# Gate and up of six FFNs as seven block products instead of eight, on one core of a Trainium2 chip

## The chip, the core and the metric

The kernel runs on one core of a Trainium2 chip. TensorE multiplies matrices into PSUM, VectorE and ScalarE work on SBUF and PSUM, GpSimd does small things, SyncE issues the DMAs. Each engine runs its own queue of instructions in order, and they meet at semaphores. The metric is the device time of one execution in microseconds, the median of the runs.

## What is computed

Two transformer blocks over x of 512 tokens x 1024, in float32: nine stages, of which six are FFNs (1, 3, 4, 6, 7, 9) and three are mixers (2: pooling and attention, 5: gated convolution, 8: Fourier and grouped attention). d_ff is 2816 in stages 1 to 6 and 2752 in 7 and 9.

```python
def rms_norm(x, g):
    xf = x.astype(jnp.float32)
    y = xf * lax.rsqrt(jnp.mean(xf * xf, axis=-1, keepdims=True) + NORM_EPS)
    return (y * g.astype(jnp.float32)).astype(x.dtype)

def swiglu(x, w_gate, w_up, w_down):
    return (jax.nn.silu(x @ w_gate) * (x @ w_up)) @ w_down
...
        x = x + 0.5 * swiglu(rms_norm(x, ffn1_norm[layer]),
                             ffn1_w_gate[layer], ffn1_w_up[layer], ffn1_w_down[layer])
```

## The kernel before

x stays in SBUF transposed (`X`: 8 tiles k of 128 channels x 512 tokens). A float32 product is made from three products of the type fp32r (`mm3`, lines 423 to 425): each operand is split into a high part (ScalarE's rounding copy: `Xh`, `wh`, `Hh`) and a low part (VectorE's subtraction: `Xl`, `wl`, `Hl`), and low x high, high x low and high x high are summed in one PSUM bank. The row factor of the norm is applied after the product: ScalarE squares the tiles of X, VectorE sums the squares into `acc`, eight one-column matmuls (line 475) add over the channels, GpSimd takes the inverse root (`r4`), two matmuls (lines 487, 488) spread it over the partitions (`rb`).

Weights come as chunks of at most 128 x 1024 elements. `weight_stream` lists them in the order of use; SyncE loads chunk n into `raw[n % 3]`, ScalarE's `high()` (line 929) and VectorE's `low()` (line 1315) split it into `wh`, `wl`. `use()` in each engine's program counts the chunks that TensorE takes and keeps the split `AHEAD = 2` chunks in front of it; the split of chunk n waits until TensorE has used chunk n-3.

An FFN (`ffn` in each program) takes hidden columns in pairs of 128. For each pair, gate and up: weights stationary, X moving with 512 tokens, 8 k tiles. The hidden comes out transposed as down needs it. VectorE multiplies gate by `rb` (line 1325), ScalarE takes the silu (line 997), VectorE multiplies up by `rb` and both, ScalarE makes `Hh` (line 960) and VectorE `Hl`. Down (`residual`) then runs over 22 hidden tiles for the 8 tiles of X, in parts of 2, 2, 2, 1 and 1 tiles (`DOWN`); behind each tile VectorE adds to X (line 1328), ScalarE makes `Xh` (957), VectorE `Xl`, and the square is summed. After the attention mixers (`mixer_out`) the tiles 4 to 7 of X come close together and their squares are summed last.

All order is written out by hand: what stands first in an engine's program is done first. `HERE` is a wait of VectorE for all of its own earlier instructions. Transposes (`turn`, line 569) are four 128-column instructions on TensorE into one bank; before, only the mixers have them. `begin(s)` waits for all engines' end of the stage before.

## Time and profile before

| | |
|---|---|
| median of 3 runs | 2712.67 us (2712.37 to 2713.19) |
| span of the profiled execution | 2710.9 us |
| TensorE, weight loads | 99%, 83% of the span |
| VectorE, ScalarE, GpSimd | 49%, 33%, 5% |
| DMA | 252.8 MB, mean 93 GB/s |

The span runs from the first to the last instruction of the profiled execution, which is one execution of its own beside the timed ones. Matmuls are pipelined: a duration of 0.39 us covers entering and leaving the array, and the pace is the distance of two starts. Lines named with an instruction are often those of a helper.

### The profile page before, as it was taken

Reading aid. Unit: us, or ns where it says so; the run is one execution under the profiler, and the core shown is the slowest. Engines: PE = TensorE matmul, PEld = TensorE weight load, DVE = VectorE, ACT = ScalarE, POOL = GpSimd, SP = SyncE. Lnnn points to the kernel's source line nnn. Section 1 sums busy time; section 2 is a strip of 40 time slices with the busy share of each in tenths; the row PEclk is TensorE's granted clock in tenths of the full one; section 3 lists DMA queues with packets and bytes.
Section 4 is the critical chain, followed back from the end, with each engine's and each line's share of the span. In section 5 each row is a group of like instructions: output and inputs, shape, how many; then the busy total and the mean of one; then the engine's idle time right before and its main releaser. Section 6 shows DMA issues by size and latency. Waiting matters only on the chain.

```text
span 2710.9 us, 31115 instructions
## 1 busy us (share of the span) xinstructions
PE 2691.8 (99%) x12443; PEld 2243.5 (83%) x12443; DVE 1339.6 (49%) x1908; ACT 900.5 (33%) x1278; POOL 136.7 (5%) x133
## 2 busy tenths in 40 slices
PE   8999999999999999999999999999999999999998
PEld 7888888888888888888888888888888888888887
DVE  5444358764443444434565444334444478644433
ACT  4232236543222332322223322223222237433221
POOL 0000004400000000000000000000000044100000
PEclk9999999999999999999999999999999999999999
DMA  4332332133332333323333233233332321233332
GB/s 158 97 99 95 94 88 74 32 96 104 96 97 92 95 104 96 100 94 94 101 93 101 94 99 96 92 97 99 99 96 93 101 84 40 71 93 93 102 101 78
DMA packets 287088, 252.81 MB, mean 93 GB/s; under 512 B 12640, under 2 KB 283744, under 8 KB 286944
## 3 DMA queue, kind: packets, MB, share of 16 engines
q1 hardware_dynamic: 286944, 250.81, 30.3%
q8 instruction: 100, 1.64, 0.2%
q14 instruction: 44, 0.36, 0.0%
HBM read 248.68 MB, written 2.10 MB: 93 GB/s over the span
## 4 chain that ended last, share of the span: by engine, by line
PE 97%; DVE 2%; ACT 0%; issue 0%; DMA 0%; SPq 0%; POOLq 0%; POOL 0%; DVEq 0%
PE bank L423 32%; PE bank L424 32%; PE bank L425 32%; PE bank L569 1%; PE bank L475 0%; DVE wl L1315 0%; PE bank L627 0%; PE bank L628 0%; DMA X<-in_xT 0%; DVE a_mx L1435 0%; PE bank L431 0%; PE bank L432 0%; DVE ft L1325 0%; DVE Xl L1328 0%; ACT wh L929 0%
## 5 line engine op out<-in xcount | busy, mean ns | idle before, releaser
L1315 DVE TENSOR_TENSOR wl<-raw,wh 128x1024 fp32r<-128x1024 f32 (+2 forms) x486 | 571.1, 1188 | 915.0 <-ACT wh L929 914.5
L423 PE MATMUL bank<-Xh,wl 128*128 128x512 f32 x2528 | 988.0, 391 | 7.6 <-DVE wl L1315 6.7
L425 PE MATMUL bank<-Xh,wh 128*128 128x512 f32 x2528 | 984.9, 390 | 0.0
L424 PE MATMUL bank<-Xl,wh 128*128 128x512 f32 x2528 | 984.7, 390 | 0.0
L929 ACT ACTIVATE wh<-raw 128x1024 fp32r<-128x1024 f32 (+2 forms) x486 | 490.9, 1024 | 946.1 <-PE bank L425 941.0
L423 PEld LDWEIGHTS bank<-Xh,wl 128*128 128x128 f32 x2528 | 474.5, 188 | 109.3 <-ACT wh L929 6.3
L425 PEld LDWEIGHTS bank<-Xh,wh 128*128 128x128 f32 x2528 | 474.4, 188 | 100.2
L424 PEld LDWEIGHTS bank<-Xl,wh 128*128 128x128 f32 x2528 | 474.6, 188 | 97.8
L423 PE MATMUL bank<-Hh,wl 128*128 128x512 f32 (+1 forms) x1061 | 408.5, 385 | 0.0
L425 PE MATMUL bank<-Hh,wh 128*128 128x512 f32 (+1 forms) x1061 | 408.3, 385 | 0.0
L424 PE MATMUL bank<-Hl,wh 128*128 128x512 f32 (+1 forms) x1061 | 408.3, 385 | 0.0
L1325 DVE TENSOR_TENSOR ft<-bank,rb 128x512 f32<-128x512 f32 x264 | 181.5, 688 | 167.4 <-PE bank L425 106.9
L425 PEld LDWEIGHTS bank<-Hh,wh 128*128 128x128 f32 x1061 | 199.3, 188 | 40.0
L423 PEld LDWEIGHTS bank<-Hh,wl 128*128 128x128 f32 x1061 | 199.3, 188 | 39.7
L424 PEld LDWEIGHTS bank<-Hl,wh 128*128 128x128 f32 x1061 | 199.3, 188 | 39.6
L960 ACT ACTIVATE Hh<-ft 128x512 fp32r<-128x512 f32 x132 | 83.4, 632 | 265.0 <-DVE ft L1325 265.0
L997 ACT ACTIVATE ft<-ft 128x512 f32<-128x512 f32 x132 | 83.5, 632 | 209.3 <-DVE ft L1325 209.2
L1325 DVE TENSOR_TENSOR Hl<-ft,Hh 128x512 fp32r<-128x512 f32 x130 | 90.0, 692 | 90.8 <-ACT Hh L960 90.8
L1325 DVE TENSOR_TENSOR ft<-ft,ft 128x512 f32<-128x512 f32 x132 | 91.4, 692 | 4.5
L957 ACT ACTIVATE Xh<-X,par 128x512 fp32r<-128x512 f32 x64 | 46.1, 722 | 123.9 <-DVE X L1328 108.0
L1971 POOL TENSOR_TENSOR r<-small,half 128x4 f32<-128x4 f32 (+1 forms) x11 | 10.5, 956 | 1368.1 <-DVE small L1334 1368.1
L1328 DVE SCALAR_TENSOR_TENSOR Xl<-X,par,Xh 128x512 fp32r<-128x512 f32 x64 | 47.8, 750 | 38.4 <-ACT Xh L957 38.4
(295 smaller groups left out, 1547.9 us busy)
## 6 DMA issues: line engine op xcount, KB each, us to landing
raw<-in_ffn_w_up SPq DMA_DIRECT2D x130, 512.0 KB, 4.0
raw<-in_ffn_w_gate SPq DMA_DIRECT2D x129, 512.0 KB, 3.6
raw<-in_ffn_w_down SPq DMA_DIRECT2D x114, 512.0 KB, 3.4
raw<-in_c_w_in SPq DMA_DIRECT2D x24, 512.0 KB, 3.7
raw<-in_w_in SPq DMA_DIRECT2D x10, 512.0 KB, 4.0
raw<-in_a_w_in SPq DMA_DIRECT2D x8, 512.0 KB, 3.7
raw<-in_a_w_out SPq DMA_DIRECT2D x8, 512.0 KB, 3.4
raw<-in_c_w_out SPq DMA_DIRECT2D x8, 512.0 KB, 3.4
```

Of the source, the lines that this page charges most:

```text
L423: e.matmul(o, ll, rh, start=start, stop=False)
L424: e.matmul(o, lh, rl, start=False, stop=False)
L425: i = e.matmul(o, lh, rh, start=False, stop=stop)
L569: e.transpose(bank[0:rows, t * 128:(t + 1) * 128], src, ident).then_inc(mm.up(name), 1)
L929: e.activation(part_of(n, wh), part_of(n, raw), ACT.Copy).then_inc(whi.up(("w", n)), 1)
L957: e.activation(Xh[:, t, :], X[:, t, :], ACT.Copy, scale=col(gain, t)).then_inc(act.up(("xh", s, t)), 1)
L960: e.activation(dst, src, ACT.Copy, scale=scale).then_inc(act.up(*names), 1)
L997: e.activation(B[0:wd, :], A[0:wd, :], ACT.Silu).then_inc(act.up(("silu", s, ht)), 1)
L1315: e.tensor_tensor(part_of(n, wl), part_of(n, raw), part_of(n, wh).bitcast(F), ALU.subtract).then_inc(wlo.up(("w", n)), 1)
L1325: e.tensor_tensor(dst, a, b, op).then_inc(dve.up(*names), 1)
L1328: e.scalar_tensor_tensor(dst, a, scalar, b, op0, op1).then_inc(dve.up(*names), 1)
L1971: e.tensor_tensor(dst, a, b, op).then_inc(pool.up(*names), 1)
```

## The change

For 2560 of the hidden columns (`GROUPED`), gate and up are one product C = A B with A = tokens x channels and B = channels x (512 gate columns, 512 up columns), five groups. A and B are cut into 2 x 2 blocks (256 tokens x 512 channels; 512 channels x 512 columns) and C is made from seven block products, D, A, B, E, B2, E2 and A2, instead of eight. The left operands are S3, the plain first block, N2, S1, a plain block, S4 and a plain block: sums of quarters of X times the gain, built at the start of each FFN (`Sf`, split into `Sh` and `Sl`). The right operands are t3, B11, t2, t1/t4, B22, B21: t1 to t4 are sums of weight blocks which VectorE makes for each half of 256 channels (`add`). Two products add on to a bank that has been read before (`again`). The operand that moves is now the weight (512 columns), the stationary one the tokens, so the hidden comes out with tokens in the partitions: VectorE and ScalarE combine the products from PSUM (U1, U2, U3, C22, C21, C12), the row factor is a scalar of the partition (`r4`), and `rb` with its two spreading matmuls is dropped in FFNs. `turn_hidden` transposes the gated hidden in blocks of 128, two blocks before the end of gate and up and the others between the matmuls of the first part of down; `Hh` and `Hl` are made from its bank. The remaining 256 (192) columns a side come first (`rest`), ordinary products with 4 token subtiles.

A unit of weights is 256 channels x 512 columns, used by 2 token subtiles (a group has 14); units of the groups have a ring of four `wh`/`wl` slots and are split three ahead, sums two further; eight raw slots hold the loads, five of them in the area of the stage, which after a mixer waits for its end (`AFTER_MIXER`). `("used", u)` is signalled behind a unit's last matmul, a product's end behind each of its two banks. The stage-wide constants of ScalarE move behind stage 1's groups.

```diff
-N_RAW = 3
-AHEAD = 2
+N_RAW = 8
+N_RING = 4
+PLAIN = (0, 1, 2)
+GROUPED = 2560

...
-FIRST = ((0, 128), (128, 256), (256, 512), (512, 1024))
+FIRST = ((0, 128), (128, 256), (256, 512), (512, 768), (768, 1024))
+REST = ((0, 256), (256, 512), (512, 768), (768, 1024))
...
+def chunks_ffn(s, wg, wu, wd):
+
+
+    got = chunks_rest(wg, wu, FIRST if s == 1 else REST)
+    for n0 in range(0, GROUPED, 512):
+        blocks = {}
+        for kh in range(2):
+            for name, w, k0 in (("B11", wg, 0), ("B12", wu, 0), ("B21", wg, 512), ("B22", wu, 512)):
+                k = k0 + 256 * kh
+                blocks[name, kh] = ([(0, (0, 512), 0, rows_of(w, k, k + 256, n0, n0 + 512))], 512, 2)
+        got.append((s, n0 == 0, blocks))
+    return got + chunks_down(wd, wg.shape[1])
...
+LOADS = (("B22", 0), ("B12", 0), ("B22", 1), ("B12", 1), ("B11", 0), ("B11", 1), ("B21", 0), ("B21", 1))
+UNITS = ("t3", "B11", "t2", "t1", "t4", "B22", "B21")
+LAST_USE = {"B11": 6, "B12": 6, "B22": 10, "B21": 12}
+LEAD = 2
+AFTER_MIXER = (3, 6, 9)
...
+        for name in UNITS:
+            for kh in range(2):
+                b11, b12, b21, b22 = (("raw", raw[b, kh]) for b in ("B11", "B12", "B21", "B22"))
+                part = ("part", kh)
+                source, total = {
+                    "t3": (part, (b22, b12, ALU.subtract)), "t2": (part, (part, b11, ALU.add)),
+                    "t1": (b12, (b12, b11, ALU.subtract)), "t4": (part, (b21, part, ALU.subtract)),
+                    "B11": (b11, None), "B22": (b22, None), "B21": (b21, None)}[name]
+                unit(512, 2, range(N_RING), 3, source, total)
+    sums = {}
+    for n, got in enumerate(units):
+        if got.sum:
+            lead = LEAD if units[n - LEAD].ahead == 3 else 0
+            sums.setdefault(n - lead, []).append(n)
+    return loads, units, release, sums
 
...
+            def turn_hidden(s, k):
+
+                rows = last_block(s) if k == 21 else 128
+                bank = take(TURNS[k % 4], ("turn", s, k))
+                w.wait_ge(par_in, 16)
+                w.wait_ge(dve, ("h", s, k // 4))
+                for t in range(4):
+                    e.transpose(bank[0:rows, 128 * t:128 * t + 128], H[:, k, t, 0:rows], ident).then_inc(
+                        mm.up(("turn", s, k)), 1)
...
+            def product(s, g, into, name, lh, ll, kh0, column, start, between=None):
+
+
+                for kh in range(2):
+                    if kh and between:
+                        between()
+                    u, h, l, _ = chunk()
+                    for i in range(2):
+                        sl = slice(column + 128 * i, column + 128 * i + 128)
+                        for kk in range(2):
+                            k, end = kh0 + 2 * kh + kk, kh == 1 and kk == 1
+                            names = [("used", u)] if kk and i else []
+                            if end:
+                                names.append((name, s, g, i))
+                            mm3(into[:, i, :], lh[:, k, sl], ll[:, k, sl], h[:, kk, :], l[:, kk, :],
+                                start and kh == 0 and kk == 0, end, *names, again=not start)
...
             def ffn(s):
...
+                rest(s)
+
+                def made(j):
+                    w.wait_ge(act, ("Sh", s, j))
+                    w.wait_ge(dve, ("Sl", s, j))
+
+                def first_turns():
+                    turn_hidden(s, 0)
+                    turn_hidden(s, 1)
+
+                for g in range(5):
+                    made(0)
+                    product(s, g, take_pair(PD, ("D", s, g)), "D", Sh[0], Sl[0], 0, 0, True)
+                    product(s, g, take_pair(PA, ("A", s, g)), "A", Xh, Xl, 0, 0, True)
+                    made(1)
+                    product(s, g, take_pair(PB, ("B", s, g)), "B", Sh[1], Sl[1], 0, 0, True)
+                    made(2)
+                    product(s, g, take_pair(PE, ("E", s, g)), "E", Sh[2], Sl[2], 0, 0, True)
+                    product(s, g, take_pair(PB, ("B2", s, g)), "B2", Xh, Xl, 4, 256, True)
+                    made(3)
+                    product(s, g, take_pair(PE, ("E2", s, g)), "E2", Sh[3], Sl[3], 0, 0, False)
+                    product(s, g, take_pair(PA, ("A2", s, g)), "A2", Xh, Xl, 4, 0, False, first_turns if g == 4 else None)
...
+                    into = [take((4 + t) % 8, ("down", s, t)) for t in range(t0, t1)]
+                    k = 0
+                    while k < 22:
+                        u, h, l, nk = chunk()
+                        for kk in range(nk):
+                            if t0 == 0 and k + 2 < 22:
+                                turn_hidden(s, k + 2)
+                            w.wait_ge(act, ("hh", s, k))
+                            w.wait_ge(dve, ("hl", s, k))
+                            for i, bank in enumerate(into):
...
             def ffn(s):
+                n = f - GROUPED
+                use(2 if s == 1 else 1)
+                if s > 1:
+                    begin(s)
+                for k in range(4):
+                    if s > 1:
+                        w.wait_ge(dve, ("x", s - 1, 4 + k))
+                    copy(Sf[2][:, k, :], X[:, 4 + k, 256:512], ("half2", s, k), scale=gain_of(s, 4 + k))
+                use()
+                for k in range(4):
+                    w.wait_ge(dve, ("S3", s))
+                    copy(Sh[0][:, k, :], Sf[0][:, k, :], ("Sh", s, 0), scale=gain_of(s, k))
+                use()
+                w.wait_ge(dve, ("N2", s))
+                copy(Sh[1][:, :, :], Sf[1][:, :, :], ("Sh", s, 1))
+                use()
+                for t in range(4):
+                    w.wait_ge(mm, ("rest", s, t))
+                    w.wait_ge(pool, ("r4", s))
+                    e.activation(U2[:, t // 2, 256 * (t % 2):256 * (t % 2) + n], banks[(6, 7, 0, 1)[t]][:, 0:n], ACT.Silu,
+                                 scale=r4[s % 2][:, t:t + 1]).then_inc(act.up(("rest", s, t)), 1)
+                w.wait_ge(dve, ("S1", s))
+                copy(Sh[2][:, :, :], Sf[2][:, :, :], ("Sh", s, 2))
+                for g in range(5):
+                    for u in range(14):
+                        use()
+                        if u == 0 and g > 0:
+                            silu_early(s, g - 1)
+                        if u == 1 and g == 0:
+                            w.wait_ge(dve, ("S4", s))
+                            copy(Sh[3][:, :, :], Sf[3][:, :, :], ("Sh", s, 3))
+                        if u == 4:
+                            w.wait_ge(dve, ("gated", s, g))
+                            for i in range(2):
+                                w.wait_ge(mm, ("A", s, g, i))
+                                copy(U2[:, i, :], pairs[PA][:, i, :], ("U1", s, g, i), ("read", ("A", s, g)))
+                        if u == 10:
+                            silu_late(s, g)
...
+            def half_of(source):
+                where, i = source
+                return (raw[loads[i].slot] if where == "raw" else part[i])[:, :]
+
+            def add(n):
+
+                a, b, op = units[n].sum
+                for where, i in (a, b):
+                    if where == "raw":
+                        w.wait_ge(raw_in[loads[i].slot], ("w", i))
+                w.wait_ge(dve, HERE)
+                e.tensor_tensor(half_of(units[n].source), half_of(a), half_of(b), op).then_inc(dve.up(("t", n)), 1)
+
             def low():
 
                 n = split[0]
-                if n == len(stream):
+                if n == len(units):
                     return
+                for m in sums_before.get(n, ()):
+                    add(m)
                 split[0] += 1
                 w.wait_ge(whi, ("w", n))
-                if n >= N_RAW:
-                    w.wait_ge(mm, ("used", n - N_RAW))
-                e.tensor_tensor(part_of(n, wl), part_of(n, raw), part_of(n, wh).bitcast(F), ALU.subtract).then_inc(
+                if units[n].before is not None:
+                    w.wait_ge(mm, ("used", units[n].before))
...
+            def gate(s, g, first):
+
+                for i in range(2):
+                    t = first + i
+                    h = H[:, 4 * g:4 * g + 4, t, :]
+                    a = (U2 if first == 0 else U3)[:, i, :].rearrange("p (k f) -> p k f", k=4)
+                    w.wait_ge(act, ("silu", s, g, t))
+                    w.wait_ge(dve, (("C12" if first == 0 else "C22"), s, g))
+                    stt(h, h, r4[s % 2][:, t:t + 1], a, ALU.mult, ALU.mult, *([("h", s, g), ("gated", s, g + 1)] if first == 0 else []))
...
+                use(2 if s == 1 else 1)
+                tt(Sf[0][:, :, :], X[:, 0:4, 0:256], X[:, 0:4, 256:512], ALU.subtract, ("S3", s))
+                for k in range(4):
+                    w.wait_ge(act, ("half2", s, k))
+                    stt(Sf[2][:, k, :], X[:, k, 256:512], gain_of(s, k), Sf[2][:, k, :], ALU.mult, ALU.add, ("S1", s))
+                use()
+                for k in range(4):
+                    w.wait_ge(act, ("Sh", s, 0))
+                    stt(Sl[0][:, k, :], Sf[0][:, k, :], gain_of(s, k), Sh[0][:, k, :].bitcast(F), ALU.mult, ALU.subtract,
+                        ("Sl", s, 0))
+                w.wait_ge(dve, ("S1", s))
+                for k in range(4):
+                    stt(Sf[1][:, k, :], X[:, k, 0:256], gain_of(s, k), Sf[2][:, k, :], ALU.mult, ALU.subtract, ("N2", s))
+                variance(small[s % 2], 2, D, ("stat", s), ("var", s))
+                use()
+                w.wait_ge(act, ("Sh", s, 1))
+                tt(Sl[1][:, :, :], Sf[1][:, :, :], Sh[1][:, :, :].bitcast(F), ALU.subtract, ("Sl", s, 1))
+                w.wait_ge(dve, ("N2", s))
+                for k in range(4):
+                    stt(Sf[3][:, k, :], X[:, 4 + k, 0:256], gain_of(s, 4 + k), Sf[1][:, k, :], ALU.mult, ALU.add, ("S4", s))
+                use()
+                w.wait_ge(act, ("Sh", s, 2))
+                tt(Sl[2][:, :, :], Sf[2][:, :, :], Sh[2][:, :, :].bitcast(F), ALU.subtract, ("Sl", s, 2))
+                w.wait_ge(pool, ("r4", s))
+                gate_rest(s, f - GROUPED)
+                w.wait_ge(act, ("Sh", s, 3))
+                tt(Sl[3][:, :, :], Sf[3][:, :, :], Sh[3][:, :, :].bitcast(F), ALU.subtract, ("Sl", s, 3))
+                for g in range(5):
+                    for u in range(14):
+                        if u == 1 and g > 0:
+                            gate(s, g - 1, 0)
+                        for i in range(2):
+                            if u == 6:
+                                w.wait_ge(act, ("U1", s, g, i))
+                                w.wait_ge(mm, ("B", s, g, i))
+                                tt(U2[:, i, :], U2[:, i, :], pairs[PB][:, i, :], ALU.subtract, ("U2", s, g, i), ("read", ("B", s, g)))
+                            if u == 7:
+                                w.wait_ge(mm, ("D", s, g, i))
+                                w.wait_ge(dve, ("U2", s, g, i))
+                                tt(U3[:, i, :], pairs[PD][:, i, :], U2[:, i, :], ALU.add, ("U3", s, g, i), ("read", ("D", s, g)))
+                            if u == 8:
+                                w.wait_ge(mm, ("E", s, g, i))
+                                w.wait_ge(dve, ("U3", s, g, i))
+                                tt(hidden(g, 2 + i), blocks(pairs[PE][:, i, :]), blocks(U3[:, i, :]), ALU.add, ("C22", s, g),
+                                   ("read", ("E", s, g)))
+                            if u == 10:
+                                w.wait_ge(mm, ("B2", s, g, i))
+                                tt(U3[:, i, :], pairs[PB][:, i, :], U3[:, i, :], ALU.add, ("C21", s, g, i), ("read", ("B2", s, g)))
+                            if u == 12:
+                                w.wait_ge(mm, ("E2", s, g, i))
+                                tt(hidden(g, i), blocks(pairs[PE][:, i, :]), blocks(U2[:, i, :]), ALU.add, ("C12", s, g),
+                                   ("read", ("E2", s, g)))
+                        use()
+                        if u == 11:
+                            gate(s, g, 2)
+                        if u == 13 and g == 4:
+                            wlo.also(("grouped", s))
+                            hidden_low(s, 0)
+                            hidden_low(s, 1)
...
+                moves, width, nk, r, before = loads[n]
+                if isinstance(before, int):
+                    kind, u = release[before]
+                    if kind == "low":
+                        w.wait_ge(whi, ("w", u))
+                        w.wait_ge(wlo, ("w", u))
+                    else:
+                        w.wait_ge(dve, ("t", u))
+                elif before:
+                    for event in (mm, act, dve, pool):
+                        w.wait_ge(event, before)
```

## Rows read from the trace of the kernel before

**Rows 1.** The page's first part: busy us, share of span, instructions by engine

```profile
PE 2691.8 (99%) x12443; PEld 2243.5 (83%) x12443; DVE 1339.6 (49%) x1908; ACT 900.5 (33%) x1278; POOL 136.7 (5%) x133
```

**Rows 2.** Waits of TensorE: who waited for whom, sum, times, longest (us)

```profile
PE bank L423 <- DVE wl L1315: 6.7, 2, 6.3
```

**Rows 3.** Chain of waits: start us, us, piece; statistics of stages 1, 3, 4

```profile
25.74 0.79 PE bank L475 x8
...
566.06 0.79 PE bank L475 x8
926.50 0.79 PE bank L475 x8
```

**Rows 4.** TensorE's timeline (start us, us, line, tiles, idle before), a 384-column stretch

```profile
503.25 0.34 PE L424 MATMUL bank<-a_KT,a_QT 96*128 96x384 f32 x1
...
503.60 0.22 PE L624 MATMUL bank<-maskR,identR 128*128 128x128 f32 x1
```

**Rows 5.** TensorE's timeline, eight transposes between matmuls

```profile
2257.60 0.60 PE L569 MATMUL bank<-par,g_qtm 128*128 128x128 f32 x4
2258.04 0.60 PE L569 MATMUL bank<-par,g_P 128*128 128x128 f32 x4
2258.39 0.47 PE L627 MATMUL bank<-g_KT,g_QS 128*128 128x512 f32 x1
2258.71 0.39 PE L628 MATMUL bank<-g_KT,g_QS 128*128 128x512 f32 x1
```

**Rows 6.** Windows of attention: all, then transposes alone (PE, PEld, last PEclk, DMA)

```profile
2256.00:2316.00 60.00, 60.00 (x397) 53.96 (x396) 49.72 (x100) 45.04 (x99) 32.74 (x21) 1.00 0.12 36
...
2256.00:2316.00 60.00, 17.17 (x120) 14.17 (x120) 1.00 0.12 36
```

**Rows 7.** Groups of VectorE's instructions by form: busy us, mean ns, idle before

```profile
L1315 DVE TENSOR_TENSOR wl<-raw,wh 128x1024 fp32r<-128x1024 f32 x445 | 539.4, 1226 | 843.6 <-ACT wh L929 843.2
L1325 DVE TENSOR_TENSOR ft<-bank,rb 128x512 f32<-128x512 f32 x260 | 178.8, 688 | 166.0 <-PE bank L425 106.9 <-ACT ft L997 56.5 <-ACT rb L960 2.6
...
L1328 DVE SCALAR_TENSOR_TENSOR Xl<-X,par,Xh 128x512 fp32r<-128x512 f32 x64 | 47.8, 750 | 38.4 <-ACT Xh L957 38.4
```

**Rows 8.** VectorE's timeline, instructions that follow each other

```profile
578.47 0.69 DVE L1325 TENSOR_TENSOR ft<-bank,rb 128x512 f32<-128x512 f32 x1 [2.13 <-ACT ft L997]
579.20 0.69 DVE L1325 TENSOR_TENSOR ft<-ft,ft 128x512 f32<-128x512 f32 x1
...
585.72 2.36 DVE L1315 TENSOR_TENSOR wl<-raw,wh 128x1024 fp32r<-128x1024 f32 x2 [0.26 <-ACT wh L929]
...
2705.05 3.22 DVE L1328 SCALAR_TENSOR_TENSOR fin<-X,par,bank 128x256 f32<-128x256 f32 x8 [0.79 <-PE bank L515]
```

**Rows 9.** ScalarE's largest group by form

```profile
L929 ACT ACTIVATE wh<-raw 128x1024 fp32r<-128x1024 f32 x445 | 462.4, 1054 | 865.3 <-PE bank L425 860.2 <-issue 3.7 <-DMA raw<-in_ffn_w_gate 0.8
```

**Rows 10.** TensorE's timeline, a late wait between matmuls in the Fourier mixer

```profile
2188.82 0.47 PE L423 MATMUL bank<-wh,Xl 128*128 128x512 f32 x1
2189.13 0.40 PE L424 MATMUL bank<-wl,Xh 128*128 128x512 f32 x1
```

**Rows 11.** DMA issues of up weights: KB each, us to landing

```profile
raw<-in_ffn_w_up SPq DMA_DIRECT2D x130, 512.0 KB, 4.0
```

**Rows 12.** VectorE's timeline, last sums of squares of stages 0, 2, 3

```profile
19.09 3.87 DVE L1325 TENSOR_TENSOR acc<-acc,sq 128x512 f32<-128x512 f32 x5
...
561.70 3.08 DVE L1325 TENSOR_TENSOR acc<-acc,sq 128x512 f32<-128x512 f32 x4
...
918.00 0.69 DVE L1325 TENSOR_TENSOR acc<-acc,sq 128x512 f32<-128x512 f32 x1
```

**Rows 13.** TensorE's timeline near the start; window behind its last matmul

```profile
7.71 0.63 PE L423 MATMUL bank<-Xh,wl 128*128 128x512 f32 x1
8.14 0.63 PE L424 MATMUL bank<-Xl,wh 128*128 128x512 f32 x1
...
2706.00:2711.00 5.00, 0.00 (x0) 0.00 (x0) 2.27 (x6) 0.00 (x0) 0.00 (x0) 0.50 0.63 210
```

384 lines of the change are left out of this document (234 added, 150 removed).

## The prediction

> **What bounds the kernel now.** I read the page's busy shares first: TensorE is busy 99% of the span and VectorE 49% [rows 1]. Then TensorE's waits: the longest cause sums to 6.7 us in two waits, 6.3 of them at the very start [rows 2], so nothing but TensorE's own work sets the end. Last its pace: stage 3 (an FFN) begins its statistics at 566.06 and stage 4 at 926.50, 360.44 us apart [rows 3]. Between them lie 1584 matmuls of 512 columns (528 each of gate, up and down), 8 one-column matmuls of 0.79 us in all and the two that spread the row factors. (360.44 - 0.79) / 1586 = 0.2268 us a matmul. The sum below is a count of TensorE instructions times this pace, plus whatever waits the new order brings. The profiled execution spans 2710.9 us; the median of the runs is 2712.67, so 1.8 us lie around the span and I add changes to the median.
>
> **Gate and up on TensorE.** Per 512 gate and 512 up columns: before 4 hidden tiles x 2 sides x 8 k x 3 = 192 matmuls; after 7 products x 2 token subtiles x 4 k x 3 = 168. Five such groups in each of six FFNs: 6 x 5 x 24 = 720 matmuls less, 720 x 0.2268 = -163.3 us. The last 256 columns a side cost 96 matmuls of 512 columns in both kernels. In stages 7 and 9 (192 columns a side) 72 of 512 become 96 of 384; at 384 columns the pitch is 0.175 (503.25 to 503.60 in two) [rows 4], 96 x 0.175 = 16.8 against 16.3: +0.5 each, +1.0. The two spreading matmuls go in each FFN: 12 x 0.2268 = -2.7. Down keeps its matmuls.
>
> **Transposes.** The hidden comes out token-major, so 22 blocks x 4 transposes of 128x128 f32 are new in each FFN, 528 in all, in TensorE's own queue. Eight of them and one matmul (L627) take from 2257.60 to 2258.71 [rows 5]: 1.11 - 0.23 = 0.88, 0.11 us each. +58.1 us. Ends: 0.087 (the second four start 0.35 before L627: 46 us) and 0.15 if switching between transposes and matmuls every few instructions costs another 0.04 (79 us); I take 0.11, which already has matmuls on both sides.
>
> TensorE's own sum: -163.3 - 2.7 + 1.0 + 58.1 = **-106.9 us**, if nothing new makes it wait.
>
> The Trainium skill ("TensorE: Matmul & The Clock Gate", Part 4, PE-mode transpose) says that transposes don't count as activity for the clock. The row disagrees in so far as it goes: 120 transposes in 60 us and the granted clock 1.00, the 2.4 GHz level [rows 6].
>
> **VectorE inside a group.** Before, a group cost it 8 low parts; now 14, 8 sums of weight blocks of the same size, 10 PSUM combinations of 512 columns and 4 gatings. A 1024-column low part lasts 1.226, a PSUM add 0.688, a three-operand one 0.750 [rows 7]. At full durations 22 x 1.226 + 10 x 0.688 + 4 x 0.750 = 36.9 us. Two instructions that don't wait for each other overlap: two low parts take 2.36, so 1.14 each (0.60 for 512 columns by the same 0.09), while one that waits for VectorE's own last result starts 0.04 after its end (578.47 + 0.69, 579.20) [rows 8]. The 8 sums wait so (0.13 more each): 22 x 1.14 + 8 x 0.13 + 10 x 0.60 + 4 x 0.66 = 34.8 us. TensorE needs 168 x 0.2268 = 38.1 us. So VectorE goes from idle half the time to 91%, but stays the shorter one. The Trainium skill ("VectorE: DVE Perf Modes", The DRAIN you can't avoid) says that the next operation doesn't start until the pipe has emptied; by that the group would be 36.9. The rows show the overlap; under either, VectorE stays below 38.1. ScalarE has 14 x 1.054 [rows 9] plus six copies or silus of 0.63, 18.5 us: no bound.
>
> Order inside the group: at unit u VectorE writes the low part of unit u+3, whose slot was freed when unit u-1 ended; it must be done three units (8.2 us) later. Walking through the 14 units with these prices, the tightest places are the second (gating 1.3, sum 1.3, low 1.1) and the eleventh; both finish 3 us or more before TensorE needs them once a group is under way. The PSUM pairs have as much: block product E is read in 1.3 us, and TensorE comes back to it two units, 5.4 us, later. The signal per bank lets the first of a pair be read 0.7 us early, off the path: nothing. I cost these at 0. A group has 14 unit boundaries on TensorE instead of 8, each with waits for both halves of the split; where a wait is met late in its queue two starts lie 0.31 apart and not 0.23 (2188.82, 2189.13) [rows 10], but the 0.2268 above is a mean over such boundaries, so 0, at most 6 x 0.08 x 30 = +14. Weight loads: same bytes, eight slots, each asked for at least five units ahead against 4.0 us to land [rows 11]: 0, except below.
>
> **The start of each FFN: a new wait.** This is what I expect to eat into the gain. In the old kernel gate and up began on Xh, Xl as they came. Now five of the seven products need sums of quarters of X, which can't be made before the last tile of X, and VectorE and ScalarE make them by turns, in the same queues as the units' split. Let T be when VectorE ends the last square sum. Its queue from there: low of rest unit 3 to T+1.1; S3 2.3; four S1 of 256 columns (8 took 3.22 [rows 8], so 1.65) 3.9; low of rest unit 4 5.1; sum t3a 6.4, its ScalarE high 7.5, low 8.7; four ScalarE copies Sh0 (about 0.4 each) 10.2; Sl0 11.9; N2 13.5; factor statistics 13.7; sum t3b 15.0, high 16.0, low 17.2; Sl1 18.4; S4 20.0; sum t2a and low B11a 22.5; Sl2 23.6; gating of the rest tiles 25.2; Sl3 26.4; sum t2b 27.6; low B11b **28.7**. TensorE wants B11b as its fourth unit. With P the start of the rest matmuls, that is P + 21.8 (96 x 0.2268) + 0.8 (statistics) + 3 x 2.72 = P + 30.8; in stages 7 and 9 P + 25.6.
> Where is T? The old trace has the same code ahead of it. After an FFN the last square sum ends at 918.69; P is 48 matmuls before the statistics, 926.50 - 10.9 = 915.6: T = P + 3.1. After an attention mixer it ends at 564.78 with P = 566.06 - 10.9 = 555.2: T = P + 9.6, because tiles 4 to 7 of X come together [rows 3, 12]. In stage 1 VectorE is free at 22.96 [rows 12] and two of the low parts are done already, so B11b is ready at 22.96 + 26.4 = 49.4. Against that TensorE: old statistics at 25.74 after 72 matmuls, new after 96: 25.74 + 5.4 + 0.8 + 8.2 = 40.1.
> The stalls: stage 1 9.3; stage 3 28.7 + 9.6 - 30.8 = 7.5; stage 4 28.7 + 3.1 - 30.8 = 1.0; stage 6 (after the conv mixer, whose last part is the same code as an FFN's) 1.0; stage 7 28.7 + 3.1 - 25.6 = 6.2, less 1 because nothing then waits for the rest tiles: 5.2; stage 9 28.7 + 9.6 - 25.6 = 12.7. Sum **+36.7 us**. After mixers the slots of the stage area are asked for only at T; each lands about 4.0 us after its issue and t3a, made at T+5.1 to 6.4, wants two: between 0 and 3 us more in stages 3, 6 and 9, in the range only. Ends: 15 (each handover 0.1 cheaper, the gating of the rest covered) and 60 (half as much again).
> The clock: TensorE ran its first 5.6 us at half speed (0.43 us between starts at 7.71 and 8.14, the 1.2 GHz level), and after its last matmul the row shows 0.50 [rows 13]. In stages 1, 3 and 9 it would now stop three or four times for 1.3 to 5 us each. Nothing in the trace shows a stop of that length in between, so: 0 to 5 us each, I take 1: +3.
>
> **Sum.** 2712.67 - 106.9 + 36.7 + 3 = 2645.5, **2646 us**, TensorE still the bound everywhere but for about 10 us at the start of each FFN.
>
> **Rivals.**
> 1. No stall at the starts: 2712.67 - 106.9 = 2606. For it: the total work of VectorE over an FFN fits. Against: the chain is a string of dependencies, and only B11b's place in it, behind Sl3 and the gating of the rest, could give way. 0.08.
> 2. VectorE is the bound in the groups too. With every instruction serial (36 gaps of 0.04 on 36.9: 38.3) and ten handovers from ScalarE or TensorE exposed by 0.1, a group takes 39.3: 30 x 1.2 = +36, 2682. For it: 91% busy leaves 3.3 us a group. Against: most waits name results that are a unit or more old. 0.15.
> 3. Slower than before: VectorE's block sums. From 38.1 + 66 / 30 = 40.3 us of VectorE a group the gain is gone. One mechanism: the eight weight sums read what a load or a split has just left and each must wait for VectorE's own queue to empty, for the load and for ScalarE's copy of the old contents of the same buffer; if the wait costs 0.9 us a sum and not 0.13 the group takes 34.8 + 6.2 = 41.0 us: 2646 + 30 x 2.9 = 2733. Against: sums are issued two units, 5.4 us, ahead of their split. 0.04.
> 4. The first down pair of each FFN, in which transposes take 0.44 of each 1.8 us, falls to the 1.2 GHz level: 132 matmuls x (0.43 - 0.227) x 6 = +161, 2807. Against: the stretch with clock 1.00 [rows 6] has about the same share of transposes (120 x 0.11 of 60 us). 0.01. This is what the Trainium skill's rule on transposes, cited above, would bring.
> 5. The change doesn't do what it says: it does, by the counts (7 x 24 against 8 x 24), so no case of its own.
>
> **How the numbers follow.** Forecast 2646, chance 0.72, with a range of its own of 2626 to 2668 (stalls 15 to 60, transposes 46 to 79, clock 0 to 15, boundaries 0 to 14, not all at one end). The whole range reaches to rival 2 and stops short of 1, 3 and 4: 2620 to 2684. A measurement here can tell 0.2%, some 5 us, from no change. Faster 0.94 (forecast, 1 and most of 2), within 0.2% 0.01, slower 0.05 (3 and 4).
>
> **What would show it.** TensorE's count down by 156 (-720 - 12 + 528, and 48 more narrow rest ones) to some 12,290 records; transposes 0.11 apart; within a group 38.1 us from one D product to the next; VectorE some 90% busy there; TensorE's waits summing to about 40 us, named by VectorE's low part or X sums, nearly all within 12 us after the rest tiles of stages 1, 3, 7 and 9, and about 1 us in 4 and 6. The prediction is wrong if TensorE waits in the middle of a group or in down, if the starts pass with no wait, or if a transpose costs 0.2 us.

## The result

The changed kernel takes **2649.11 us** (median, 2647.59 to 2651.26) against 2712.86 for the kernel before on the same chip: ratio 0.9766, 95% interval 0.9752 to 0.9779, 2.3% faster. Forecast 2646, range 2620 to 2684. The profiled execution spans 2645.5 us against 2710.9 [rows 1], 65.4 less where the sum had 67.2 less. Of all executions timed for this document one took a slower course, 2896.3 us at a mean granted clock of 0.849 (banks moved for all four pairs, below; its three others: 0.994 to 0.995), and it is left out of that version's time.

The page's busy times (us, share of the span, instructions) and, from its part 4, the shares of the chain that ended last:

```profile
PE 2598.1 (98%) x12287; PEld 2168.7 (82%) x12287; DVE 1882.5 (71%) x2481; ACT 1157.2 (44%) x1591; POOL 136.9 (5%) x133
...
PE 90%; DVE 6%; ACT 2%; issue 1%; DMA 1%; SPq 0%; DVEq 0%; POOLq 0%; POOL 0%; ACTq 0%
```

TensorE has 156 records fewer [rows 1], the count of the prediction to the last one. It is still the bound, but 6% of the chain now runs over VectorE. Where, the waits of TensorE tell (who waited for whom: sum, times, longest in us):

```profile
PE pair L522 <- DVE wl L1572: 18.1, 10, 3.6
PE pair L522 <- ACT Xh L1144: 7.4, 1, 7.4
PE pair L522 <- DVE X L1582: 5.5, 2, 3.7
PE pair L522 <- ACT wh L1113: 2.2, 1, 2.2
PE pair L522 <- issue: 1.9, 2, 1.3
```

L522 is the first matmul of a split product (L423 before), L1572 VectorE's low part (L1315 before). The 7.4 us at the very start stand against 6.3 in [rows 2]; all the others are new. By place, as TensorE's timeline has them: stage 1 1.25, 2.40, 0.70, 3.34; stage 3 3.66, 1.80; stage 4 0.54; stage 6 0.57; stage 7 0.84, 3.55; stage 9 1.89, 0.67, 2.42, 2.22, 1.96. Together 27.8 us, all within the first units of an FFN. There are none in the middle of a group or in down.

**The group.** Two windows in stage 3, one group's length each (D products start at 615.35 and 653.43; us, then busy us and instructions of TensorE, its weight loads, VectorE, ScalarE, GpSimd, then granted clock, DMA share, GB/s):

```profile
629.90:668.00 38.10, 38.10 (x170) 31.55 (x169) 34.54 (x36) 18.24 (x21) 0.00 (x0) 1.00 0.39 111
668.00:706.10 38.10, 38.10 (x170) 31.55 (x169) 34.44 (x36) 18.24 (x21) 0.00 (x0) 1.00 0.40 111
```

TensorE 38.1 (forecast 38.1), VectorE 34.5 (34.8), ScalarE 18.2 (18.5), at full clock. VectorE's busy time counts overlapped instructions once, which is why it is less than 22 x 1.22 and the rest added up. A low part and the weight sum behind it, in the same group:

```profile
652.50 1.22 DVE L1572 TENSOR_TENSOR wl<-raw,wh 128x1024 fp32r<-128x1024 f32 x1
653.63 1.22 DVE L1559 TENSOR_TENSOR part<-part,raw 128x1024 f32<-128x1024 f32 x1
```

**The transposes.** TensorE's timeline in the down stage of stage 3 (start, us, count):

```profile
770.41 0.60 PE L644 MATMUL pair<-par,H 128*128 128x128 f32 x4
770.76 0.47 PE L522 MATMUL pair<-Hh,wl 128*128 128x512 f32 x1
771.07 0.39 PE L523 MATMUL pair<-Hl,wh 128*128 128x512 f32 x1
...
803.28 0.60 PE L644 MATMUL pair<-par,H 128*128 128x128 f32 x4
```

From the first of these sets to the last are 18 steps of six matmuls and four transposes, 1.826 us each: 1.826 - 6 x 0.2268 = 0.465, so 0.116 a transpose. [rows 5] gave 0.11 with eight in a row. The difference is what follows a set: its first matmul and the second start 0.31 us apart and not 0.23 (770.76, 771.07), and here that is paid for every four transposes, there for eight.

**One whole FFN.** The statistics of stages 3 and 4 (answering [rows 3], there 360.44 apart):

```profile
563.36 0.95 PE L571 MATMUL pair<-ones,acc 128*128 128x1 f32 x8
...
908.47 0.95 PE L571 MATMUL pair<-ones,acc 128*128 128x1 f32 x8
```

345.11 us apart, 15.3 less. By the prices of the prediction TensorE's own part is -120 x 0.2268 - 2 x 0.2268 + 88 x 0.11 = -18.0; the stop at 585.31 below costs 1.96 from start to start (2.19 - 0.23); 0.7 us are left over. Of these the transposes at 0.116 are 0.55.

### The profile page after: what moved, and what is told of

Read it like the earlier page. It is cut to its first block, busy times and chain, and to the rows that moved or that the text cites. A ratio compares the mean times of both kernels' runs of the same rounds, so it can differ in the third digit from the quotient of the medians.

```text
span 2645.5 us, 32342 instructions
## 1 busy us (share of the span) xinstructions
PE 2598.1 (98%) x12287; PEld 2168.7 (82%) x12287; DVE 1882.5 (71%) x2481; ACT 1157.2 (44%) x1591; POOL 136.9 (5%) x133
## 4 chain that ended last, share of the span: by engine, by line
PE 90%; DVE 6%; ACT 2%; issue 1%; DMA 1%; SPq 0%; DVEq 0%; POOLq 0%; POOL 0%; ACTq 0%
PE pair L522 29%; PE pair L524 28%; PE pair L523 28%; PE pair L644 2%; DVE wl L1572 1%; PE pair L749 1%; DMA raw<-in_ffn_w_up 1%; DVE Sf L1585 1%; DVE Sl L1582 1%; ACT wh L1113 1%; DVE part L1559 0%; DVE acc L1582 0%; DVE Xl L1585 0%; ACT Sh L1144 0%; DVE X L1582 0%
## 5 line engine op out<-in xcount | busy, mean ns | idle before, releaser
L1572 DVE TENSOR_TENSOR wl<-raw,wh 128x1024 fp32r<-128x1024 f32 (+2 forms) x487 | 575.7, 1185 | 436.6 <-ACT wh L1113 436.2
L522 PE MATMUL pair<-Hh,wl 128*128 128x512 f32 (+1 forms) x1061 | 420.2, 396 | 0.0
L524 PE MATMUL pair<-Hh,wh 128*128 128x512 f32 (+1 forms) x1061 | 409.3, 386 | 0.0
L523 PE MATMUL pair<-Hl,wh 128*128 128x512 f32 (+1 forms) x1061 | 408.8, 385 | 0.0
L522 PE MATMUL pair<-wh,Xl 128*128 128x512 f32 (+2 forms) x976 | 377.9, 387 | 28.5 <-DVE wl L1572 13.3
L522 PE MATMUL pair<-wh,Sl 128*128 128x512 f32 x960 | 374.7, 390 | 6.7 <-DVE wl L1572 4.8
L524 PE MATMUL pair<-wh,Xh 128*128 128x512 f32 (+2 forms) x976 | 375.6, 385 | 0.0
L523 PE MATMUL pair<-wl,Xh 128*128 128x512 f32 (+2 forms) x976 | 375.4, 385 | 0.0
L523 PE MATMUL pair<-wl,Sh 128*128 128x512 f32 x960 | 374.0, 390 | 0.0
L524 PE MATMUL pair<-wh,Sh 128*128 128x512 f32 x960 | 374.0, 390 | 0.0
L1572 DVE TENSOR_TENSOR wl<-part,wh 128x1024 fp32r<-128x1024 f32 x180 | 219.7, 1221 | 65.6 <-ACT wh L1113 65.2
L522 PEld LDWEIGHTS pair<-wh,Xl 128*128 128x128 f32 x976 | 184.8, 189 | 67.3 <-ACT wh L1113 21.6
L522 PEld LDWEIGHTS pair<-Hh,wl 128*128 128x128 f32 x1061 | 199.6, 188 | 35.6
L522 PEld LDWEIGHTS pair<-wh,Sl 128*128 128x128 f32 x960 | 180.7, 188 | 45.6 <-issue 8.2
```

The costliest lines, as they stand in the source:

```text
L522: e.matmul(o, ll, rh, start=start, stop=False, skip_group_check=again)
L523: e.matmul(o, lh, rl, start=False, stop=False, skip_group_check=again)
L524: i = e.matmul(o, lh, rh, start=False, stop=stop, skip_group_check=again)
L1572: e.tensor_tensor(part_of(n, wl), source_of(n), part_of(n, wh).bitcast(F), ALU.subtract).then_inc(wlo.up(("w", n)), 1)
```

## Where TensorE stops

Stage 3 on TensorE (start, us, idle before and its releaser):

```profile
550.86 0.80 PE L522 MATMUL pair<-wh,Xl 128*128 128x512 f32 x1 [3.66 <-DVE X L1582]
551.45 0.63 PE L523 MATMUL pair<-wl,Xh 128*128 128x512 f32 x1
551.88 0.63 PE L524 MATMUL pair<-wh,Xh 128*128 128x512 f32 x1
...
583.12 0.39 PE L524 MATMUL pair<-wh,Xh 128*128 128x512 f32 x1
585.31 0.47 PE L522 MATMUL pair<-wh,Xl 128*128 128x512 f32 x1 [1.80 <-DVE wl L1572]
585.62 0.39 PE L523 MATMUL pair<-wl,Xh 128*128 128x512 f32 x1
585.85 0.40 PE L524 MATMUL pair<-wh,Xh 128*128 128x512 f32 x1
```

and on VectorE, from its last square sum (which ended at 557.10) to the low part for which the second stop waits:

```profile
557.26 1.23 DVE L1572 TENSOR_TENSOR wl<-raw,wh 128x1024 fp32r<-128x1024 f32 x1 [0.16 <-ACT wh L1113]
...
562.69 1.23 DVE L1559 TENSOR_TENSOR part<-raw,raw 128x1024 f32<-128x1024 f32 x1 [0.35 <-DMA raw<-in_ffn_w_up]
565.04 1.23 DVE L1572 TENSOR_TENSOR wl<-part,wh 128x1024 fp32r<-128x1024 f32 x1 [1.12 <-ACT wh L1113]
...
577.64 1.22 DVE L1572 TENSOR_TENSOR wl<-raw,wh 128x1024 fp32r<-128x1024 f32 x1
578.78 1.22 DVE L1582 TENSOR_TENSOR Sl<-Sf,Sh 128x1024 fp32r<-128x1024 f32 x1
579.91 1.66 DVE L1585 SCALAR_TENSOR_TENSOR H<-pair,r,U 128x256 f32<-128x256 f32 x4
581.49 1.21 DVE L1582 TENSOR_TENSOR Sl<-Sf,Sh 128x1024 fp32r<-128x1024 f32 x1
582.80 1.23 DVE L1559 TENSOR_TENSOR part<-part,raw 128x1024 f32<-128x1024 f32 x1
583.94 1.22 DVE L1572 TENSOR_TENSOR wl<-raw,wh 128x1024 fp32r<-128x1024 f32 x1
```

How to read it: B11a and B11b are the two units (halves of 256 channels) of the weight block B11, t2b is the second unit of the weight sum t2, and Sl2 and Sl3 are the low parts of the sums S1 and S4 (the third and fourth that are built). At 577.64 the low part of B11a is made. Then come Sl2, the gating of the rest tiles, Sl3 and the sum t2b, and only at 583.94 the low part of B11b, which ends at 585.16; TensorE resumes at 585.31. From the last square sum that is 28.1 us, where the prediction's chain has 28.7. The wait for loads after a mixer, which the prediction had as 0 to 3 us in its range only, is the 0.35 us at 562.69 (0.95 in stage 9). Whether B11b waits for its place in the queue or its product for the sums of X can't be told from these rows alone, as both are made in that queue. The experiments tell it.

The first stop, 3.66 us before the first rest matmul, was not foreseen.

## The experiments

Ratios are against the kernel before, timed in the same call.

**Is it the sums, or the queue?** First the four products with sums of X were fed with X itself, so that this kernel and the next compute something else and serve for their time only:

```diff
-                    w.wait_ge(act, ("Sh", s, j))
-                    w.wait_ge(dve, ("Sl", s, j))
...
-                    product(s, g, take_pair(PD, ("D", s, g)), "D", Sh[0], Sl[0], 0, 0, True)
+                    product(s, g, take_pair(PD, ("D", s, g)), "D", Xh, Xl, 0, 0, True)
```

(and B, E, E2 alike)

> The changed kernel, but the four block products with a sum of quarters of X (D, B, E, E2) take Xh and Xl as left operands, of the same shapes, so the product is another one; VectorE and ScalarE still make all the sums at their old places in the queues, only TensorE no longer waits for them. Theory A (queue): TensorE's stops at the starts come from the low part of B11b and of t3b, which stand behind the sums and the gating in VectorE's queue, so they stay where they are: some 2645 to 2650 us, stops of 1.8 us in stage 3 and 3.6 in stage 7 named by the low part. Theory B (dependency): TensorE waits for the sums themselves; then the stops go, about 20 us of the measured 27.8 (the 5.5 us after the mixers' down stay): 2629 us or less.

Measured 2649.71 us, ratio 0.9764 (0.9748 to 0.9780): the changed kernel's time. The waits of TensorE, and its stop in stage 3:

```profile
PE pair L522 <- DVE wl L1571: 28.8, 10, 7.3
...
587.02 0.47 PE L522 MATMUL pair<-wh,Xl 128*128 128x512 f32 x1 [1.76 <-DVE wl L1571]
```

(28.8 with the 7.3 of the kernel's start, which is named by the low part here.) With no product left that needs a sum of X, stage 3 stops for 1.76 us as before. In stage 1 the stops of 1.25 and 0.70 are gone, but those that remain are 4.42 and 3.11, 7.5 in sum against 7.7. In stage 9 the four stops behind the first become two of 3.22 and 3.33. The stops don't need a sum of X as operand: it is the place in the queue, and theory B falls.

Then the sums of X were not made at all:

```diff
-                tt(Sf[0][:, :, :], X[:, 0:4, 0:256], X[:, 0:4, 256:512], ALU.subtract, ("S3", s))
...
-                    copy(Sh[0][:, k, :], Sf[0][:, k, :], ("Sh", s, 0), scale=gain_of(s, k))
...
-                tt(Sl[3][:, :, :], Sf[3][:, :, :], Sh[3][:, :, :].bitcast(F), ALU.subtract, ("Sl", s, 3))
```

> As the run with the sums made but unused, and now VectorE and ScalarE don't make the sums of quarters of X either (left out: Sf, Sh, Sl, their four sums, splits and differences, 17 VectorE instructions at each start). Theory A: the chain from the last square sum to the low part of B11b is shorter by S3 1.2, S1 1.6, Sl0 1.7, N2 1.6, Sl1 1.2, S4 1.6, Sl2 1.1, Sl3 1.2 and the wait for Sh0, some 12 to 14 us, more than any stop: all stops by the low part go, and only the two waits for a PSUM bank after the mixers' down (3.7 + 1.9) stay: 2649 - 22 - about 3 for the slower pace behind each stop = 2622 to 2627 us. If the stops have another cause (transposes, clock, weight loads), they stay: above 2640.

Measured 2616.41 us, ratio 0.9643 (0.9629 to 0.9658), 32.7 less than the changed kernel. The waits:

```profile
PE pair L522 <- DVE X L1567: 5.6, 2, 3.7
...
PE pair L522 <- DVE wl L1557: 0.7, 1, 0.7
```

The stops by the low part go but for 0.7 us in stage 9, the two others stay, as theory A says; the time is 6 us below its range. What I had put too low is the pace around the stops. Each costs 0.16 us more from start to start than its idle time says (583.12 to 585.31 is 2.19, less one pitch 1.96, against 1.80), some 2 us in all; and behind several of them TensorE runs at half speed for a while (below): the changed kernel has 20 such starts, 0.2 us each, at 39.4, 2315.6 and 2322.3, this one none there: 4 us. With the 21.5 us of idle time that went these make 27.5 of the 31.1 by which the span is shorter; another 1.2 are half-speed starts in the Fourier mixer that this profile happens not to have, and 2 us stay unexplained.

**What a transpose costs.**

```diff
-                for t in range(4):
+                for t in (0, 1, 2, 3, 0, 1, 2, 3):
```

> The changed kernel with every transpose of the down stage issued twice into the same PSUM place (528 more). Theory: a transpose costs TensorE 0.11 us and nothing else: +58 us, 2707; by the prediction's ends +46 to +79, 2695 to 2728. If transposes made the clock fall when they are more frequent, the down stretch with two sets (0.9 us in 2.3) would show a granted clock below 1.00 and the cost would be over 100 us.

Measured 2707.84 us, ratio 0.9981 (0.9972 to 0.9990), 58.7 more than the changed kernel: 58.7 / 528 = 0.111 us. A window with two sets of transposes every 2.26 us (the same columns as in the windows above):

```profile
770.00:800.00 30.00, 30.00 (x180) 25.80 (x179) 16.01 (x21) 12.25 (x18) 0.00 (x0) 1.00 0.25 80
```

The granted clock is 1.00. Here 8 x 0.11 of each 2.26 us, 39% of TensorE's time, go to transposes and the clock stays at 2.4 GHz; rival 4 has nothing left. The Trainium skill ("TensorE: Matmul & The Clock Gate", Part 4, PE-mode transpose) says that they don't count as activity; this row neither confirms nor contradicts the rule, as there are matmuls between all sets, but it shows that the rule costs nothing here. The four additional transposes stand directly behind four others, which is why they come out at 0.111 and the sets of the changed kernel at 0.116.

**How much has VectorE to spare in a group?** Five additional low parts in each group, then two:

```diff
+                if place_of[n] in (2, 4, 6, 12, 13):
+                    tt(part_of(n, wl), source_of(n), part_of(n, wh).bitcast(F), ALU.subtract)
+                    w.wait_ge(dve, HERE)
```

> The changed kernel with five additional 1024-column low parts a group on VectorE, each a repetition of the one before it and waited for by VectorE itself (1.27 us each, 6.3 a group). Theory: VectorE has 38.1 - 34.5 = 3.6 us a group to spare, so a group becomes 40.8 us long and VectorE its bound: 30 x 2.7 = +81 us less what the starts hide, 2720 to 2740. Rival 2 in its strong form (VectorE is already the bound, no time to spare): +30 x 6.3 = +190, 2840. If VectorE's own work in a group were much shorter than read: no change, 2649.

Measured 2711.13 us, ratio 0.9993 (0.9984 to 1.0003): all of the gain is gone, though it is 9 us less than the least that I expected. Two starts of a B product, one group apart, and VectorE between them (L1589 is the repetition, L1579 the low part itself, L1563 a weight sum):

```profile
681.75 0.47 PE L522 MATMUL pair<-wh,Sl 128*128 128x512 f32 x1 [1.54 <-DVE wl L1579]
...
683.79 1.22 DVE L1563 TENSOR_TENSOR part<-raw,part 128x1024 f32<-128x1024 f32 x1
684.93 1.22 DVE L1589 TENSOR_TENSOR wl<-raw,wh 128x1024 fp32r<-128x1024 f32 x1
686.18 1.23 DVE L1579 TENSOR_TENSOR wl<-raw,wh 128x1024 fp32r<-128x1024 f32 x1
...
722.00 0.47 PE L522 MATMUL pair<-wh,Sl 128*128 128x512 f32 x1 [1.52 <-DVE wl L1579]
```

A group takes 40.25 us, with one stop of 1.5 us and shorter ones, for VectorE. I had 40.8. A repetition costs what I had for it, as the low part behind it waits for it: 1.25 us (684.93 to 686.18). It is VectorE's own work that is shorter: 40.25 - 5 x 1.25 = 34.0 us when its instructions follow each other without a gap, not the 34.5 of the windows above, where some of them stand alone behind a wait and overlap with none before. The trace has 24 such stops, of 1.1 to 1.6 us. From the first B product of a stage to its fifth they make 48.4 of the 62 us in the six stages (160.1 or 161.0 us a stage in place of 152.3 to 152.5); the rest is in the starts, where some stops are longer, too. With two:

> The changed kernel with two additional 1024-column low parts a group on VectorE (each a repetition of the one before it). With five of them a group took 40.25 us and VectorE was its bound, so its own work without them is 40.25 - 5 x 1.14 to 1.23 = 34.1 to 34.6, and with two of them 36.4 to 37.0. Theory (VectorE has 3.6 us a group to spare and spends them freely): the group stays at 38.1, only the starts and first groups may lose up to 2.3 us where VectorE is behind: 2649 to 2655. Rival 2 of the prediction (VectorE bound): 30 x 2.4 = 72 us more, 2720.

Measured 2651.66 us, ratio 0.9776 (0.9759 to 0.9792). A group in its window, and a new stop of the first group:

```profile
630.83:668.93 38.10, 38.10 (x170) 31.55 (x169) 37.22 (x39) 18.22 (x20) 0.00 (x0) 1.00 0.40 111
...
589.78 0.47 PE L522 MATMUL pair<-wh,Sl 128*128 128x512 f32 x1 [0.56 <-DVE wl L1579]
```

VectorE is busy 37.2 of 38.1 us and TensorE doesn't wait. Only in the first group there is a new stop of 0.5 to 0.6 us, in stages 1, 3, 4 and 6, 2.8 us in all from start to start, while the stop of 1.80 us in stage 3 shrinks to 0.62; the 2.5 us between the medians are within what half-speed starts make from one profile to the next (11 more here, 2.2 us). Rival 2 (72 us more) is out: VectorE is free up to TensorE's 38.1, and beyond it its work counts. The changed kernel has 3.6 us of it left a group by its busy time, 4.1 by the run with five.

**The signal per bank and the order by subtile.**

```diff
-                    for i in range(2):
-                        sl = slice(column + 128 * i, column + 128 * i + 128)
-                        for kk in range(2):
+                    for kk in range(2):
+                        for i in range(2):
+                            sl = slice(column + 128 * i, column + 128 * i + 128)
...
-                            if end:
-                                names.append((name, s, g, i))
+                            if end and i:
+                                names += [(name, s, g, 0), (name, s, g, 1)]
```

> Undoes two named parts of the change: each product gives one signal for both PSUM banks, and the two token subtiles alternate inside a weight block row instead of one after the other. Theory (VectorE has a unit or more in hand at every product): 2649, within 2 us; the last product of a group is read 0.7 us later and down starts no later. Rival (the signal per bank and the order by subtile carry part of the gain): the second bank's reader starts up to 0.7 + 1.4 us late in each product, 7 products x 30 groups, and if a third of it showed, +100 us.

Measured 2649.39 us, ratio 0.9768 (0.9753 to 0.9782), no difference. These two parts of the change are worth nothing here. That the gain is the seven products rests on the counts and on the group's 38.1 us; what the ring of four slots, the eight raw slots and the sums two units ahead are worth no run shows.

**B11b's low part earlier in the queue.**

```diff
                 use()
+                use()
+                w.wait_ge(pool, ("r4", s))
+                gate_rest(s, f - GROUPED)
                 w.wait_ge(act, ("Sh", s, 2))
                 tt(Sl[2][:, :, :], Sf[2][:, :, :], Sh[2][:, :, :].bitcast(F), ALU.subtract, ("Sl", s, 2))
-                w.wait_ge(pool, ("r4", s))
-                gate_rest(s, f - GROUPED)
...
-                        use()
+                        if g > 0 or u > 0:
+                            use()
```

(use() makes the next unit's split; the second one, new here, is that of B11b. Sl3 goes behind the fourth unit.)

> The changed kernel with the sum t2b and the split of B11b moved ahead of Sl2 and the gating of the rest tiles in VectorE's and ScalarE's queues, and Sl3 to the fourth unit. Theory (the stop is the place of B11b's low part in VectorE's queue): that low part ends 1.1 + 1.6 + 1.1 = 3.8 us earlier, but units 1 to 3 wait for Sh2, Sl1 and t3b that aren't moved, and Sl2 and the gating then come late for B12 and the next units: the fourth stop shrinks by up to 3.8 us in each stage where it is the only one (1.8, 0.5, 0.6 in stages 3, 4, 6 go) and by 1 to 3 in stages 1, 7 and 9: 5 to 12 us less, 2637 to 2644. If TensorE waited for the X sums instead, nothing would be won: 2649 or more.

Measured 2639.59 us, ratio 0.9733 (0.9718 to 0.9747), 9.5 less than the changed kernel. In stage 3 only the first stop is left,

```profile
549.58 0.61 PE L522 MATMUL pair<-wh,Xl 128*128 128x512 f32 x1 [3.66 <-DVE X L1584]
...
1787.70 0.47 PE L522 MATMUL pair<-wh,Sl 128*128 128x512 f32 x1 [1.91 <-DVE wl L1574]
```

in stages 4 and 6 none, and in stage 7 the stop of 3.55 has become one of 1.91, one unit later. That is the time expected (2637 to 2644). The same instructions in another order, so again the queue.

**The stop after the mixers' down.** The rest tiles take PSUM banks 6, 7, 0 and 1 at once. In the changed kernel the last output tiles of the attention mixers lie in bank 6 (tile 7 of stage 2, tile 6 of stage 8), and it is free only when VectorE has added them to X: theory A of the next runs. First try:

```diff
-                    among = range(2) if pair == 2 else range(8)
+                    among = range(2) if pair == 2 else range(2, 6) if pair == 3 else range(8)
```

> The changed kernel with the last pair of output tiles of the two attention mixers kept in PSUM banks 2 to 5, so that the rest tiles of the FFN behind them, which take banks 6, 7, 0 and 1 at once, don't wait until VectorE has read the mixer's last tiles. Theory: the two waits of 3.7 and 1.9 us at the start of stages 3 and 9 go; P comes that much earlier, but the chain of VectorE that ends with B11b's low part hangs on the last square sum and not on P, so the later stops of stages 3 and 9 grow by up to as much: between 5.5 us less (2643.5) and no change (2649), nearest to no change. If the bank wait also delayed the chain, the whole 5.5 us are won.

Measured 2650.98 us, ratio 0.9774 (0.9759 to 0.9788), the stop of 3.66 unchanged and that of stage 9 up from 1.89 to 3.17. This tells nothing on the theory, as the edit did not do what I meant: of banks 2 to 5 only bank 3 was free when stage 2 placed its last pair, so tile 7 stayed in 6, and in stage 8 tile 7 took the place of tile 6 there, and tile 7 is read 1.3 us later. The second try places all four pairs:

```diff
+                    among = ((0, 1, 6, 7), (0, 1, 6, 7), (6,), range(2, 6))[pair]
```

> The earlier run for banks left tile 7 of the first mixer in bank 6, because no bank of 2 to 5 was free when it was placed, and its stop of 3.66 us stayed. Here the first two pairs of the mixers' output tiles get banks 0, 1, 6, 7, tile 4 of the second attention mixer bank 6, and tiles 5 to 7 banks 2 to 5. Theory A (the stop is the wait for a PSUM bank): the stops of 3.7 and 1.9 us before the rest tiles of stages 3 and 9 go or fall below 1 us; but VectorE's chain hangs on its last square sum, not on the start of the rest tiles, so the later stop of stage 3 grows from 1.8 to about 5 us and those of stage 9 by about 1.9: 2646 to 2650. Theory B (the rest tiles wait for X itself): both stops stay.

Measured 2651.71 us, ratio 0.9778 (0.9762 to 0.9794), 1.7 above the range. In stage 3:

```profile
576.57 0.47 PE L522 MATMUL pair<-wh,Sl 128*128 128x512 f32 x1 [0.75 <-DVE wl L1572]
581.75 0.47 PE L522 MATMUL pair<-wh,Xl 128*128 128x512 f32 x1 [2.18 <-DVE wl L1572]
588.05 0.47 PE L522 MATMUL pair<-wh,Xl 128*128 128x512 f32 x1 [1.72 <-DVE wl L1572]
```

The rest tiles start without a stop, so it was the bank. And nothing is won: 4.65 us of stops now come later in place of 3.66 + 1.80. TensorE arrives earlier at the same low parts, which hang on VectorE's last square sum. Stage 9 is alike (8.7 us of stops in place of 9.2). A stop of 0.95 us is new in the attention of stage 2 (523.34), and the profile has 14 half-speed starts more, 2.8 us; these are most of the 4.4 us by which its profiled span is longer than the changed kernel's.

**The start in another order.** All that VectorE and ScalarE do at a start, ordered by when TensorE needs it, with the first try's banks:

```diff
+                if s > 1:
+                    low()
+                add(first_unit[s])
...
+                add(first_unit[s] + 1)
+                low()
...
                 tt(Sl[1][:, :, :], Sf[1][:, :, :], Sh[1][:, :, :].bitcast(F), ALU.subtract, ("Sl", s, 1))
...
+                variance(small[s % 2], 2, D, ("stat", s), ("var", s))
+                use(3)
```

> The changed kernel with the start of each FFN in another order on VectorE and ScalarE: block sums t3a and t3b before the sums of X, the splits of B21a and B21b and of t3a ahead of Sl0, t2a, t2b and both B11 splits before Sl2, the gating of the rest tiles and Sl3; and the mixers' last tiles in other banks, as in the run for banks. Theory: each low part then ends 3 to 8 us earlier than now, so that stages 3, 4, 6 have no stop, stage 7 less than 1 us, stage 1 1.5 and stage 9 about 5: 2649 - 25 to 28 = 2621 to 2624. Rival: the work at the start is the same in sum, and what is put later (Sl2, Sl3, gating) is late in its turn: 2635 or more.

Measured 2630.22 us, ratio 0.9696 (0.9680 to 0.9712), 18.9 less than the changed kernel, 6 short of what I expected. Stages 4, 6 and 7 don't stop. Left are 3.15 in stage 1, 3.67 in stage 3, 3.17 and 1.88 in stage 9: the bank stops that the first try didn't remove, and in stage 1 the wait for Sl0, which now stands behind two weight sums. With the banks of the second try:

> The run with the reordered start (2630.2) with the banks really moved. Its stage 3 had no stop after the one of 3.67 us, its stage 9 one of 1.88 after one of 3.17. Theory: the low parts have a few us in hand there, so most of 3.67 + 3.17 is won, and the half-speed starts behind the first (13 of 0.43, 2.6 us) too: 2621 to 2627. If nothing is in hand, the stops only move: 2630.

Measured 2627.4 us, ratio 0.9687 (0.9673 to 0.9702), the fastest version that computes the reference, 0.8% under the changed kernel; 0.4 us outside my range, and 2.8 less than with the first try's banks. The stops themselves only moved: 11.9 us in the six starts before, 11.7 here, and the new one of 0.96 us in the attention of stage 2. What went are half-speed starts, such as the 13 behind the 3.67 us of stage 3, 2.6 us. The stops came back where low parts and sums of X are late:

```profile
PE pair L524 <- DVE wl L1577: 10.8, 5, 7.0
PE pair L524 <- DVE Sl L1590: 7.1, 2, 3.9
```

(The lines are two further down in this kernel; 7.0 of the first is the kernel's start.) Stage 9 has one long stop now, 3.88 us for Sl0. Between this run and the one that makes no sums (2616.4) 11 us remain.

## Why the prediction was right, point by point

- **The count times the pace:** right. 156 records less, 0.2268 us a matmul, 38.1 a group, one FFN as worked out within 0.7 us. Those 0.7 are nearly all in the next term; the handovers, costed at 0 with an end of +14, leave 0.15 an FFN.
- **Transposes:** mis-sized by a little. The trace has 0.116 each in sets of four, 528 x 0.1163 = 61.4 us where the term had 58.1, and doubling them gives 0.111 for those that follow others. I had read 0.11 from eight in a row, which spreads the later start of the matmul behind a set over eight and not four. The ends, 0.087 and 0.15, were needlessly wide.
- **VectorE in a group:** 34.5 against 34.8, and the runs with more low parts confirm both that it is no bound and where it would be one (rival 3 put the end of the gain at 40.3 us a group; it was gone at 40.25). What I took from [rows 8], that instructions that don't wait for each other overlap by 0.09, holds here throughout: low parts of 1.22 us start 1.14 behind the instruction before them. So do the weight sums that stand behind a low part, six of the eight of a group (652.50 to 653.63); only the two behind a combination or a gating start 0.04 to 0.13 after its end, so that of the 0.13 us that I added for each sum (8 x 0.13 = 1.0) little is there. The reason is in the program: `HERE` is not a wait for all of VectorE's earlier instructions, but for those that signal its main semaphore; low parts signal another (`wlo`), so a sum doesn't wait for them. The Trainium skill ("VectorE: DVE Perf Modes", The DRAIN you can't avoid) says that the next operation doesn't start until the pipe empties, which gave 36.9; the trace doesn't agree with that. The same section adds that an operation that isn't held starts earlier, and with that it agrees (1.14 us from start to start at 1.22 us each).
- **The stall at the starts:** the term was +36.7, and 27.8 us of idle time were found. By stage, forecast and found: 9.3 and 7.7; 7.5 and 5.5; 1.0 and 0.5; 1.0 and 0.6; 5.2 and 4.4; 12.7 and 9.2. The chain of VectorE was read to 0.6 us (28.1 against 28.7), and its cause, the place of B11b behind Sl3 and the gating, is the one that rival 1 names; making no sums and moving B11b both show it. From start to start the stops cost 30.3 us (the gaps less one pitch each), the kernel's own start 1.1 more. The place was right for most of them, "within 12 us after the rest tiles" not for all: the last stops of stages 1, 7 and 9 come 17, 13 and 17 us after them, and two stand before them (next point). And 25.6 us, the way to B11b in stages 7 and 9, adds up to 25.8 (16.8 + 0.8 + 8.2).
- **The bank after the mixers:** missed. I took the rest tiles to start as soon as the mixer's matmuls end; they wait 3.7 and 1.9 us for bank 6. This wait stood in no term. It did not change the sum, since TensorE would else have waited for the low parts: the forecast for stage 3 was 7.5, the two stops together cost 5.8 from start to start, and 1.2 are in the half-speed starts between them.
- **The clock:** +3 forecast for 0 to 5 us in each of stages 1, 3 and 9; found 26 starts at 0.43, 5.2 us, and 6 more in the Fourier mixer, 1.2 us, behind stops of 1.39 and 0.60. Right in kind, low in size, and blind to that last place: the kernel before has the same two stops (1.38 and 0.60 at 2254.42 and 2255.64) with full pace behind them, so "nothing in the trace shows a stop of that length in between" was not quite so.
- **Together:** -106.9 + 30.3 + 1.1 + 6.4 + 3.3 = -65.8, against -65.4 measured (3.3 for the transposes). The stalls were put 6.4 us too high, clock, start and transposes together 7.8 too low, so that the forecast lies as near as it does is in part luck: the terms are right in kind, and their errors cancel. Of the 3.6 us between the sum (2645.5) and the median 1.8 are in the spans; for the rest, the median of the runs lies 3.6 above the profiled span here, and 1.8 in the kernel before.
- **Rivals:** 1 (no stall) is what the version without sums reaches, 2616 with the bank stops still in it; 2, 3 and 4 are out by the group's 38.1 us, by a weight sum that costs 1.23 us with a wait of 0.13 at most in a group, and by the clock.
